# Expert weight slots: router weights in the parameter tile, repacked mixer buffers, nine slots in the last stage

## The reference, cut to what matters

```python
def hier_moe(xf, w_rg, b_rg, w_re, b_re, w1, w3, w2):
    g_logits = xr @ w_rg + b_rg            # 4 groups
    e_logits = xr @ w_re + b_re            # 32 experts, 8 in a group
    ...                                    # best group, its two best experts, gates
    def expert_block(args):
        xblk, e = args
        return (jax.nn.silu(xblk @ w1[e]) * (xblk @ w3[e])) @ w2[e]
    ...
def second_block(x, c, ctx, ...):
    for layer in range(2):
        ...                                # layer 0: even_mixer; layer 1: window_attention
        # layer 0: hier_moe over 512 rows (tokens and context), layer 1: over the 256 tokens
```

## Time and profile before

| what | value |
|---|---|
| median of 3 runs | 2274.24 us (2269.87 to 2276.2) |
| the profiled execution's own time | 2264.46 us |
| its span, first to last instruction | 2262.6 us, mean granted clock 0.984 |
| TensorE busy | 2153.8 us (95%) |
| VectorE busy | 882.4 us (39%) |
| moved by DMA | 612 MB, mean 270 GB/s |
| chain that ended last | PE 91%, ACT 3%, DVE 3% |

### The profile page before, as it was taken

The page is one execution under the profiler, slowest core; times in us unless marked ns, Lnnn a source line. Parts: engine busy times, 40 slices in busy tenths (PEclk is TensorE's granted clock), DMA queues, the critical chain, the costliest instruction groups (busy, mean ns, idle before and its releaser), DMA issues.

```text
span 2262.6 us, 21849 instructions
## 1 busy us (share of the span) xinstructions
PE 2153.8 (95%) x8991; PEld 1129.6 (50%) x8991; DVE 882.4 (39%) x1623; ACT 314.9 (14%) x686; POOL 46.6 (2%) x62
## 2 busy tenths in 40 slices
PE   7999999998999999999899999999899899989898
PEld 4557766455577764444633333333345543333333
DVE  3336665326365654022432333323575422121122
ACT  2221001215310003000100000000134100000000
POOL 0000000000000000000100000000000000000000
PEclk9999999998999999999899999999999899999999
DMA  9347766350276675121899999999320899999995
GB/s 356 119 149 260 260 238 232 124 186 34 81 261 226 243 269 186 40 74 38 349 424 418 413 411 418 414 413 394 130 76 1 350 427 425 427 428 426 427 427 243
DMA packets 142532, 612.00 MB, mean 270 GB/s; under 512 B 15320, under 2 KB 66200, under 8 KB 117728
## 3 DMA queue, kind: packets, MB, share of 16 engines
q1 hardware_dynamic: 135328, 596.07, 66.7%
q0 software_dynamic: 7008, 14.40, 1.8%
q10 hardware_dynamic: 96, 0.10, 0.0%
HBM read 616.07 MB, written 4.33 MB: 274 GB/s over the span
## 4 chain that ended last, share of the span: by engine, by line
PE 91%; ACT 3%; DVE 3%; issue 2%; DMA 1%; SPq 0%; ACTq 0%; DVEq 0%
PE psum L2058 19%; PE psum L494 14%; PE psum L981 13%; PE psum L2078 10%; PE psum L2091 8%; PE psum L956 6%; PE psum L1559 4%; PE psum L534 3%; PE psum L2031 1%; PE psum L969 1%; PE psum L607 1%; PE psum L2068 1%; PE psum L480 1%; ACT consts L2253 1%; PE psum L1695 1%
## 5 line engine op out<-in xcount | busy, mean ns | idle before, releaser
L981 PE MATMUL psum<-normed_t,ring 128*128 128x256 f32 x1408 | 305.5, 379 | 0.0
L981 PEld LDWEIGHTS psum<-normed_t,ring 128*128 128x128 f32 x1408 | 267.5, 190 | 40.6 <-issue 4.3
L494 PE MATMUL psum<-ring,normed_t 128*128 128x512 f32 (+1 forms) x672 | 267.0, 557 | 9.9 <-DVE small L447 2.5
L886 DVE SCALAR_TENSOR_TENSOR arena<-ring,silu_c,arena 128x1024 f32<-128x1024 f32 x168 | 204.5, 1278 | 0.0
L494 PEld LDWEIGHTS psum<-ring,normed_t 128*128 128x128 f32 x672 | 124.3, 200 | 142.5 <-issue 140.9
L2078 PE MATMUL psum<-ring,consts 128*64 128x512 f32 x640 | 169.8, 594 | 21.5 <-ACT consts L2253 19.7
L2416 DVE TENSOR_TENSOR scaled<-scaled,psum 128x512 f32<-128x512 f32 x32 | 22.0, 687 | 426.8 <-PE psum L2058 426.8
L2091 PE MATMUL psum<-consts 128*128 128x512 f32 x384 | 186.1, 606 | 1.1 <-DVE small L447 0.2
L2058 PE MATMUL psum<-ring,arena 128*64 128x512 f32 x640 | 173.4, 609 | 9.7 <-issue 9.2
L2058 PE MATMUL psum<-ring,consts 128*64 128x512 f32 x640 | 168.4, 593 | 6.8 <-issue 6.8
L2411 DVE TENSOR_TENSOR resid<-resid,psum 128x512 f32<-128x512 f32 x192 | 131.8, 687 | 48.2 <-PE psum L2091 48.2
(11 more groups left out here) (398 smaller groups left out, 2217.0 us busy)
## 6 DMA issues: line engine op xcount, KB each, us to landing
ring<-in_w SPq DMA_DIRECT2D x120, 2048.0 KB, 18.0
arena<-in_w SPq DMA_DIRECT2D x48, 2048.0 KB, 19.6
ring<-in_w_mod SPq DMA_DIRECT2D x24, 2048.0 KB, 8.1
normed_t<-in_w SPq DMA_DIRECT2D x24, 2048.0 KB, 21.0
ring<-in_ffn_w_up SPq DMA_DIRECT2D x44, 1024.0 KB, 9.4
ring<-in_ffn_w_down SPq DMA_DIRECT2D x10, 2048.0 KB, 9.4
ring<-in_ab_w_in SPq DMA_DIRECT2D x6, 2048.0 KB, 17.3
ring<-in_ple_w_gate SPq DMA_DIRECT2D x4, 2048.0 KB, 9.5
```

Source lines behind the costliest of these rows:

```text
L494: m = te.eng.matmul(PS[:, bank, 0:n], src[:, k0 + k, P * t:P * t + P], w[:, k, :], start=(k == 0), stop=(k == kc - 1))
L886: ins = dv.scalar_tensor_tensor(out=acc, in0=w, scalar=sc, in1=acc, op0=ALU.mult, op1=ALU.add)
L981: m = pe.matmul(PS[:, b, 256 * hf:256 * hf + 256], w[:, hf, k, P * cc:P * cc + P], HT[:, k, 0:T], start=(k == 0), stop=(k == KC - 1))
```

## The change

1. **Router weights outside the ring.** The router tiles leave `stream`. Both layers' router weights go to columns 0 to 287 of the parameter tile `PRM` (constants of the first block, no longer read), by `load_router` on SP. The seventh place of the experts, which the router tile had, belongs to a mixer tile now.
2. **Mixer buffers packed.** In em, EFX moves down to 6160 and EY up to 8192 to 12287, so that mid is free when the last Fourier piece is copied (em.fy7), and top when em's last output tile is used (em.out1.used) instead of when the residual is added. In at, mid and top wait for at.y3, the last attention output on DVE, instead of at.res11. The order of places is rewritten to the order in which they come free.
3. **A ninth slot in moe1** over the constants (`DEAD[:, 0:4096]`), from moe0.end on. moe1's scratch moves to the context rows of `X` and to the second gate row of `GB`; for that, layer 1 loads only one gate row.

No arithmetic, and no order on PE, DVE or ACT, is changed.

```diff
@@ the stream of ring tiles
-        def router_tile(i):
-            wtile(f"moe{i}.r", (... w_router_g_2 ...), (... w_router_e_2 ...))
...
-        if on("moe0"):
-            router_tile(0)
         moe_at = {0: len(stream)}
...
-        if on("out"):
-            router_tile(1)
         moe_at[1] = len(stream)
@@ the even mixer's buffers in the arena Z
-        EY = Z[:, 6160:10256].rearrange("p (c t) -> p c t", c=8)
-        EFX = Z[:, 10256:11280].rearrange("p (b n) -> p b n", b=2)
+        EFX = Z[:, 6160:7184].rearrange("p (b n) -> p b n", b=2)
+        EY = Z[:, 8192:12288].rearrange("p (c t) -> p c t", c=8)
@@ the attention's residual
-            dv.wait_ge(gate_loaded[2], 32)
+            dv.wait_ge(gate_loaded[2], 16)
@@ scratch of the expert stages
-        YW = [DEAD[:, 0:1024], DEAD[:, 1024:2048]]
-        XT = ... DEAD[:, 2048:2560], DEAD[:, 2560:3072] / Z[:, 3072:3584], Z[:, 3584:4096]
-        HGT = DEAD[:, 3072:3584].rearrange("p (j r) -> p j r", j=4)
-        PICK = DEAD[:, 3584:4096].rearrange("p (t n) -> p t n", t=4)
+        ROUTER = PRM[:, 0:288].rearrange("p (k n) -> p k n", k=8)
@@ Experts.__init__
-                self.slots = [slots[slot_of[n]] for n in self.owners[:4]] + [Z[:, 4096:8192], Z[:, 8192:12288], slots[slot_of[self.owners[4]]], HTF]
+                own = [slots[slot_of[n]] for n in self.owners]
+                mid, top = Z[:, 4096:8192], Z[:, 8192:12288]
+                x2, x3, g1 = X[:, 2, :], X[:, 3, :], GB[:, 1, :]
+                if nt == 4:
+                    self.homes = ["own0", "own1", "own2", "mid", "own3", "top", "own4", "normed"]
+                    self.slots = [own[0], own[1], own[2], mid, own[3], top, own[4], HTF]
+                    self.YW = [DEAD[:, 0:1024], DEAD[:, 1024:2048]]
+                    self.turned, self.hidden_t, self.pick_at = DEAD[:, 2048:3072], DEAD[:, 3072:3584], DEAD[:, 3584:4096]
+                else:
+                    self.homes = ["dead", "own0", "own1", "own2", "mid", "top", "own3", "own4", "normed"]
+                    self.slots = [DEAD[:, 0:4096], own[0], own[1], own[2], mid, top, own[3], own[4], HTF]
+                    self.YW = [x2, g1[:, 768:896]]
+                    self.turned, self.hidden_t, self.pick_at = x3, g1[:, 0:512], g1[:, 512:768]
+                self.ns = len(self.slots)
@@ Experts.load_weights (MSLOTS became self.ns everywhere)
-                elif i < 4:
-                    freed(sp, self.owners[i])
-                elif i < 6:
-                    sp.wait_ge(sems["dve"], upto("dve", self.before))
-                elif i == 6:
-                    freed(sp, self.owners[4])
+                elif home == "dead":
+                    sp.wait_ge(sems["dve"], upto("dve", "moe0.end"))
+                elif home == "normed":
+                    sp.wait_ge(sems["pe"], upto("pe", f"{self.L}.xmt{self.nt - 1}1"))
+                elif home == "mid":
+                    sp.wait_ge(sems["dve"], upto("dve", "em.fy7" if self.nt == 4 else "at.y3"))
+                elif home == "top" and self.nt == 4:
+                    sp.wait_ge(sems["pe"], upto("pe", "em.out1.used"))
+                elif home == "top":
+                    sp.wait_ge(sems["dve"], upto("dve", "at.y3"))
                 else:
-                    sp.wait_ge(sems["pe"], upto("pe", f"{self.L}.xmt{self.nt - 1}1"))
+                    freed(sp, self.owners[int(home[3])])
+            def load_router(self, sp):
+                sp.wait_ge(sems["dve"], upto("dve", "moe0.end" if self.l else "ple1.res11"))
+                sp.dma_start(ROUTER[:, :, 0:4], a["w_router_g_2"][self.l].rearrange("(p k) n -> p k n", k=KC)).then_inc(self.router_in, 16)
+                sp.dma_start(ROUTER[:, :, 4:36], a["w_router_e_2"][self.l].rearrange("(p k) n -> p k n", k=KC)).then_inc(self.router_in, 16)
@@ Experts.sp, the ring tiles of the attention
-                    sp.wait_ge(sems["pe"], upto("pe", self.done_with(6 * PAIRS - MSLOTS + i)))
+                    sp.wait_ge(sems["pe"], upto("pe", self.done_with(6 * PAIRS - self.ns + self.homes.index(f"own{i}"))))
@@ gate_rows, and the DVE wait for them
-            for r in range(2):
+            for r in range(2 - layer):
@@ the program of SyncE
+                moe[0].load_router(sp)
                 moe[0].sp(sp, stream[moe_at[0]:moe_at[1]])
...
+                moe[1].load_router(sp)
                 moe[1].sp(sp, [])
```

More of the change, by code:

```diff
@@ L1923, in __init__ @@
                 s = lambda n: sem(f"{L}_{n}")
-                self.w_loaded = [s(f"weights{i}_loaded") for i in range(MSLOTS)]
+                self.router_in = s("router_loaded")
                 self.xm_written = s("inputs_written")
@@ L1940, in __init__ @@
                 self.owners = sorted((n for n in before_moe[layer]), key=[n for n, _ in stream].index)
-                self.slots = [slots[slot_of[n]] for n in self.owners[:4]] + [Z[:, 4096:8192], Z[:, 8192:12288], slots[slot_of[self.owners[4]]], HTF]
-                self.o_slots = [self.slots[i] for i in (4, 5, 7)]
-                self.OXM = self.slots[6].rearrange("p (t n) -> p t n", t=4)
+                own = [slots[slot_of[n]] for n in self.owners]
[12 more added lines that the diff above has]
+                self.ns = len(self.slots)
+                self.w_loaded = [s(f"weights{i}_loaded") for i in range(self.ns)]
+                four = lambda v: v.rearrange("p (j r) -> p j r", j=4)
+                self.XT = [[four(self.turned[:, 0:512]), four(self.turned[:, 512:1024])], [four(Z[:, 3072:3584]), four(Z[:, 3584:4096])]]
+                self.HGT = four(self.hidden_t)
+                self.PICK = self.pick_at.rearrange("p (t n) -> p t n", t=nt)
+                self.OTG, self.OSL, self.OUT = self.hidden_t, self.turned[:, 0:512], self.turned[:, 512:1024]
+                self.o_slots = [mid, top, HTF]
+                self.OXM = own[4].rearrange("p (t n) -> p t n", t=4)
                 self.OS = Z[:, 0:CAP * nt].rearrange("p (t r) -> p t r", t=nt)
@@ L1970, in slot @@
             def slot(self, c, q, h):
-                return self.slots[(6 * c + 2 * q + h) % MSLOTS]
+                return self.slots[(6 * c + 2 * q + h) % self.ns]
             def loaded(self, pe, c, q):
@@ L2090, in pe_combine @@
                         pe.wait_ge(sems["dve"], upto("dve", f"{L}.add{i - 2}.{c}"))
-                    m = pe.matmul(PS[:, 4 + i % 2, :], PICK[:, t, :], YW[t // 2][:, 512 * n:512 * n + 512], start=True, stop=True)
+                    m = pe.matmul(PS[:, 4 + i % 2, :], self.PICK[:, t, :], self.YW[t // 2][:, 512 * n:512 * n + 512], start=True, stop=True)
                     p.step(m, f"{L}.sum{i}.{c}")
@@ L2107, in logits @@
                 def logits(t):
-                    rows(te, f"{L}.r", t, 4 + t, ("dve", f"{L}.lg{t}"), n=36, last=t == self.nt - 1)
+                    te.take(4 + t, "dve", f"{L}.lg{t}")
+                    pe.wait_ge(sems["dve"], upto("dve", f"n.{L}.ht{t}"))
+                    pe.wait_ge(self.router_in, 32)
+                    for k in range(KC):
+                        m = pe.matmul(PS[:, 4 + t, 0:36], HT[:, k, P * t:P * t + P], ROUTER[:, k, :], start=k == 0, stop=k == KC - 1)
+                    p.step(m, f"{L}.r.t{t}")
                 def token_rows(t):
@@ L2423, in dve @@
                         p.settle()
-                        dv.wait_ge(gate_loaded[1 + 2 * l], 32)
+                        dv.wait_ge(gate_loaded[1 + 2 * l], 32 - 16 * l)
                     else:
```

50 lines of the change are left out of this document (22 added, 28 removed).

## The result

| kernel | median us | lowest to highest | profiled execution | its span |
|---|---|---|---|---|
| before | 2272.73 | 2269.87 to 2276.2, 4 runs | 2264.46 | 2262.6 |
| changed | 2257.47 | 2254.16 to 2259.05, 4 runs | 2259.05 | 2257.2 |

The changed kernel takes 0.9934 of the time before (95% interval 0.9922 to 0.9946): 15.3 us less, where 9.4 were predicted. Both kernels timed again later gave the same: 2256.73 us against 2271.99, ratio 0.9935 (0.9921 to 0.9949).

A forecast was written before the change was run, and what follows sets the result against it. The prediction took moe0 as bound by PE and late moe1 by the DMA engines' weight stream. Gains of 7.0 us in moe1 and 2.4 in moe0 took the median from 2274.24 to 2264.8 us, range 2258 to 2273.

The forecast's parts named there:

- What bounds the kernel: moe0 is bound by PE; moe1 from about 1890 us on by the DMA engines, with 33.4 us of weight stalls.
- how far ahead the stream is: In moe1, tile 9 was to land 6.4 us earlier and tile 11 7.6 earlier, the lead then staying.
- Part 1: moe1: ninth slot and early loads put nine tiles in place before the first refill, starting the stream sooner: -7.0 us.
- Part 2: moe0: earlier written rows and gather remove PE's 2.36 us wait at the turn of pair 1: -2.4 us.
- The sum: Whole kernel: -7.0 and -2.4 give 2255.1 us profiled, 2264.8 us as median, 0.41% faster.
- the carry-over: Whole kernel: the median's 9.8 us above the profiled execution was assumed to stay after the change.
- Part 3: Router loads, new SP waits, a later attention tile, fewer gate rows and moved scratch were to cost nothing.
- The slower ninth place: moe1: the odd-column slot over the constants takes writes more slowly; at half speed 40 us net, 2314; chance 0.05.
- It doesn't do what it says: moe1: with eight slots filled early the first refill lands only 0.9 us sooner, 2273.3 us; chance 0.02.
- Half of it: moe1's lead is only one tile, 4.9 us, or moe0's wait stays: 2269.3 us, range -2 to -6.8; chance 0.24.
- More: moe1's slow matmuls after the last wait vanish too, plus 1.1 us more lead: about -13, 2261 us; chance 0.05.

The follow-up runs named there:

- last_only: Kernel before with only the moe1 part of the change (nine slots, early loads), moe0 as before: 2266.13 us against 2271.49, ratio 0.9976.
- before_again: The kernel before, unchanged, timed and profiled a second time: 2272.18 us against 2271.49, ratio 1.0007.
- nine_late_arena: Changed kernel, but in moe1 mid and top load after at.res11, behind the ring slots; nine slots stay: 2258.46 us, before beside it 2271.36.
- first_only: Kernel before with only the moe0 part (router tile, packed mixer buffers, slot order), moe1 as before: 2263.68 us against 2271.49, ratio 0.9972.
- writes_first: Kernel before, with SP holding moe0's seventh and eighth weight loads until POOL's four writes have landed: 2263.75 us against 2271.36, ratio 0.9966.
- late_gather: Changed kernel, with POOL's first moe0 gather held until hid1 of pair 0 is done: 2264.67 us, before beside it 2271.36.
- fill_short: Kernel before with 12 useless matmuls on PE ahead of moe0's turn of pair 1: 2269.93 us against 2271.99, ratio 0.9993.
- eight_slots: Changed kernel without moe1's ninth slot, its scratch back over the constants, two gate rows loaded: 2262.84 us, before beside it 2271.49.
- new_again: The changed kernel, unchanged, timed and profiled again: 2256.73 us against 2271.99 for the kernel before, ratio 0.9935.

## Why the prediction came out as it did

**What bounds the kernel, and how far ahead the stream is: right.** Counted from moe1's first combine (1828.26 in the first profile, 1829.29 after), tile 9 landed at -24.7 us after, -18.3 before, and tile 11 at -14.9 against -7.3: leads of 6.4 and 7.6, the figures of the text to the tenth. The last tile landed 408.0 to 408.3 after that combine in the five profiles with nine slots and whole refills; in the six where moe1 is the old one, 414.4 to 415.5. The lead is kept to the end: 7.0 us at the mean. DMA share stayed at 1.00. One small thing was off: the first long stall came two pairs later, not one (1987.2 against 1932.6).

**Part 1, -7.0 us: right.** With the moe0 part already there, it is worth -15.3 - (-7.8) = -7.5 us; alone (last_only) -5.4, where its profile shows the same landing (408.0) and attention took 1.4 us more than in before_again. The restart costs what the idle-engine row said: 7.9 us. What the text had from the Trainium skill ("DMA: Bandwidth & Descriptors", "Anatomy of one DMA"), an estimate of 6.8 us for this load, does not hold for this queue; the new row repeats 7.9. The text's lower bound, 4.9 for one tile alone, is what the ninth slot gave (4.9 in the landings). The other 2.4 us are there, but not for the reason that the text gives: the early arena loads are not needed for them (nine_late_arena lands the same).

**Part 2, -2.4 us with bounds 0 and 2.4: this step failed.** Its mechanism was right: earlier writes, an earlier gather, no wait at the turn. The writes landed 2.9 to 9.9 us after their issue instead of 11.0 to 15.5 in before_again. The group of the four writes in the changed kernel:

```profile
DMA to landing us min/median/max: 2.9/6.4/9.9
```

The last of them was in at 1110.5 (I had "about 1107"), the gather went out at 1111.4 (I had "near 1109"), landed in 4.4 us, and nothing took the wait's place. But its size was read from one execution, and both bounds with it. In before_again the wait is 5.07, the clock behind it costs 4.56, and against that stand 2.0 us lost later: 7.6 net, where first_only measured 7.8 and writes_first 7.6. The upper bound had no room for any of this, although 1114.51 for the gather and 1115.31 for the refill stood 0.8 us apart in the first profile. I had the rows, and the question "what if the two come closer or in the other order" was not asked.

**The sum: the carry-over hid the same error.** "The median of the runs is 9.8 above the profiled execution; I carry that over." A constant is carried over only if the change does not touch its cause. Before's profiled execution was quick by the shorter wait and the full clock: (5.07 - 2.36) + 4.56 = 7.3 us, and 2264.46 + 7.3 = 2271.7, near the median of the later runs (2271.99). That it comes so near is partly luck: before_again's own profiled execution took 2269.99, only 5.5 us more than the first, since it also ran at full clock behind the last wait of moe1, where the first had lost 1.7 us, and smaller differences lie elsewhere. The change removes that very place, and after's profile lies on top of its runs (2259.05 and 2256.08 us profiled, medians 2257.47 and 2256.73). With the typical wait the sum would have been -7.0 - 7.6 = -14.6, near the 15.3 measured.

**Part 3, costs nothing: right but for 2 us that it had no reason to see.** From the first combine of pair 16 back to that of moe0's last pair, attention and what lies around it took 227.33 and 227.48 us in the two profiles of before, and 227.34 in late_gather; in the ten other profiles it took 228.9 to 229.6. The granted clock tells where. Windows of the changed kernel at two places, behind the end of moe0 and ahead of moe1:

```profile
1613.40:1616.80 3.40, 3.40 (x5) 1.35 (x4) 0.00 (x0) 0.00 (x0) 0.00 (x0) 0.50 1.05 379
1770.40:1787.50 17.10, 12.69 (x57) 11.81 (x58) 7.54 (x32) 3.05 (x6) 1.08 (x2) 0.50 0.72 254
```

And of before_again at the same two:

```profile
1620.60:1624.00 3.40, 3.40 (x9) 1.52 (x8) 0.00 (x0) 0.00 (x0) 0.00 (x0) 1.00 0.22 65
1778.70:1792.40 13.70, 10.35 (x47) 9.87 (x48) 5.65 (x30) 2.78 (x5) 0.53 (x1) 0.50 1.01 408
```

The first place stands behind a PE wait of 2.4 us that every profile has. In all ten slower ones the clock is at 0.50 for some 3.4 us behind it or behind the next wait, 1.7 us of work; in the three quick ones it stays at 1.00. At the second place the low clock lasts 17.1 us instead of 13.7 in seven of the ten, those at 229.4 to 229.6. It isn't the new loads: writes_first and fill_short, which load nothing early, show both. Nor is it simply the clock at moe0's start: last_only had that drop and still took 228.9, and the first profile of before had none and took 227.3. What decides it stays open.

**Rivals.** The slower ninth place is refuted: with one tile in nine going there, tiles 20 to 50 of moe1 took 150.9 us after and 150.2 in before_again, tiles 50 to 90 200.7 and 200.6. "It doesn't do what it says" gave eight slots 0.9 us. The medians are 0.8 apart, but that they agree is luck: the stream of eight_slots ends 2.4 us sooner than first_only's, since the text compared tile 8 alone (1.1 us) and the lead grows to 2.8 at tile 11. "Half of it" fell with both terms. "More" (-13) came nearest in size for the wrong reason: the slow matmuls after the last wait (8.78 us) are still there in the first profile of the changed kernel and gone in new_again (7.1), and before_again did not have them either, so the change does not decide them.

## What to carry to other kernels

Where two engines issue DMAs within a us of each other, the profile shows one outcome of a race; price the bad one too, and ask for the whole echo: the wait, the lower clock behind it and the matmuls that run in it. If the profiled execution is faster than all timed runs, look for such a place before carrying the difference over, since the change may remove its cause. And small writes that a later gather needs want empty engines: holding two large loads back by 9 and 15 us brought half of what the whole change brought.

## What the runs showed of the hardware

- A gather of token rows issued 0.05 us behind a refill of weights took 11.8 us to land, 0.1 us ahead of it 12.3 us, 0.8 us ahead 9.9 us, and 5.5 us ahead, on quiet engines, 4.4 us. Its place in time against the other queue's loads decides, not its size.
- After a wait of 5.1 to 5.5 us of PE (before_again, last_only, late_gather) the granted clock was 0.50 for another 9 to 11 us, and the matmuls that take 10.0 us took 14.6 in before_again and 13.9 in last_only. After the wait of 2.36 us in the first profile it was not seen; after waits of 2.0 to 2.7 us in moe1 it was seen after some and not after others.
- Twelve idle matmuls kept it at 1.00 at that place, at the cost of their own 5.45 us, which the wait covered.
- 2 MB tiles written from column 1797 of the constants on moved as fast as the others: tiles 50 to 90 took 200.7 us with them and 200.6 without.
